# Expert stage of a two-layer encoder trunk: a narrower table of column widths, 4439 columns a layer in place of 4612

## The reference

```
h   = rms_norm(x, norm_mix[l])
x   = x + concat(attention(h), pooling(h), retention(h)) @ w_out[l]
x   = x + moe_ffn(rms_norm(x, norm_ffn[l]), router, w_gate[l], w_up[l], w_down[l])
```

```
layer 0: 127 | 162 157 155 153 153 150 148 142 142 141 139 133 130 130 128 128 127 125 125 113 113 111 111 111 110 110 110 104 104 104 100
layer 1: 137 | 167 167 162 151 150 148 147 144 141 141 138 135 134 130 129 128 128 123 119 118 116 114 113 113 105 104 104 103  98  96  93
```

## Time and profile before

| | |
|---|---|
| median of the runs | 3310.61 us |
| span of the profiled execution | 3312.4 us |
| TensorE busy | 3164.2 us, 96% |
| expert stage, layer 0, first expert matmul to the last one's end | 880.24 to 1650.61 us |
| expert stage, layer 1 | 2529.05 to 3298.26 us |
| HBM read, written | 545.90 MB, 80.35 MB |

### The profile page before, as it was taken

The page is one execution under the profiler, slowest core; times in us unless marked ns, Lnnn a source line. Parts: engine busy times, 40 slices in busy tenths (PEclk is TensorE's granted clock), DMA queues, the critical chain, the costliest instruction groups (busy, mean ns, idle before and its releaser), DMA issues.

```text
span 3312.4 us, 58893 instructions
## 1 busy us (share of the span) xinstructions
PE 3164.2 (96%) x20244; PEld 2476.5 (75%) x20244; DVE 1483.7 (45%) x4546; ACT 627.8 (19%) x1812; POOL 1239.4 (37%) x1346
## 2 busy tenths in 40 slices
PE   7999999998699999999989999999987999999998
PEld 4555556555599999999945565565556999999998
DVE  3576676766322222222236766766763222222221
ACT  4122222222011111111142222221221111111111
POOL 1221321322255545554322322322212554555544
PEclk9999999998899999999989999999988999999999
DMA  7212222123488999999942122122134889999996
GB/s 276 71 55 83 64 62 83 53 73 112 155 277 285 312 306 338 321 339 341 295 146 83 42 83 83 42 83 79 46 125 179 277 282 307 310 335 331 327 342 191
DMA packets 245905, 629.12 MB, mean 190 GB/s; under 512 B 65644, under 2 KB 137836, under 8 KB 212796
## 3 DMA queue, kind: packets, MB, share of 16 engines
q1 hardware_dynamic: 183004, 542.50, 46.1%
q0 software_dynamic: 62592, 82.75, 11.4%
HBM read 545.90 MB, written 80.35 MB: 189 GB/s over the span
## 4 chain that ended last, share of the span: by engine, by line
PE 80%; DMA 6%; DVE 5%; issue 3%; DVEq 2%; ACT 1%; POOL 1%; SPq 1%; ACTq 0%; POOLq 0%
PE bank L1419 23%; PE bank L1226 17%; PE bank L1447 15%; PE bank L1387 12%; DMA arena<-hrows,arena 3%; PE bank L1217 3%; PE bank L1220 3%; PE bank L1190 2%; DVE arena L1135 1%; PE bank L1343 1%; PE bank L1364 1%; PE bank L1288 1%; DMA out<-arena 1%; DMA wts<-in_w_in 1%; DMA arena<-out 1%
## 5 line engine op out<-in xcount | busy, mean ns | idle before, releaser
L1419 PE MATMUL bank<-arena,wts 128*128 128x135 f32 (+6 forms) x8192 | 1023.5, 287 | 3.5 <-ACTq L797 3.5
L1419 PEld LDWEIGHTS bank<-arena,wts 128*128 128x128 f32 x8192 | 1017.1, 191 | 3.7 <-issue 3.7
L1226 PE MATMUL bank<-wts,arena 128*128 128x512 f32 x1536 | 695.1, 599 | 42.2 <-DVEq L879 19.4
L656 POOL DMA_INDIRECT out<-arena x316 | 503.6, 1594 | 204.8 <-ACT arena L806 117.6
L1226 PEld LDWEIGHTS bank<-wts,arena 128*128 128x128 f32 x1536 | 281.9, 192 | 345.5 <-issue 321.2
L1447 PE MATMUL bank<-arena,wts 128*128 128x135 f32 (+6 forms) x4096 | 517.0, 287 | 16.5 <-DVE arena L1168 16.4
L1447 PEld LDWEIGHTS bank<-arena,wts 128*128 128x128 f32 x4096 | 509.3, 190 | 19.7 <-issue 19.7
L1387 PE MATMUL bank<-wts,arena 128*128 128x512 f32 x1024 | 454.5, 597 | 0.0
L646 POOL DMA_INDIRECT arena<-hrows,arena x304 | 296.3, 975 | 187.1 <-issue 169.8
L1387 PEld LDWEIGHTS bank<-wts,arena 128*128 128x128 f32 x1024 | 193.3, 191 | 231.0 <-issue 215.6
L1135 DVE STREAM_TRANSPOSE arena<-arena 128x256 f32<-128x256 f32 x304 | 135.4, 445 | 506.8 <-DMA arena<-hrows,arena 486.5
(11 more groups left out here) (191 smaller groups left out, 2834.2 us busy)
## 6 DMA issues: line engine op xcount, KB each, us to landing
wts<-in_w_gate SPq DMA_DIRECT2D x128, 1024.0 KB, 8.0
wts<-in_w_up SPq DMA_DIRECT2D x128, 1024.0 KB, 10.7
wts<-in_w_down SPq DMA_DIRECT2D x128, 1024.0 KB, 16.0
arena<-out SPq DMA_DIRECT2D x184, 128.0 KB, 3.0
hrows<-arena SPq DMA_DIRECT2D x36, 512.0 KB, 3.9
out<-arena SPq DMA_DIRECT2D x36, 512.0 KB, 2.7
arena<-in_x SPq DMA_DIRECT2D x32, 512.0 KB, 7.0
wts<-in_w_in SPq DMA_DIRECT2D x8, 2048.0 KB, 13.7
```

The lines of the kernel that those rows point to most:

```text
L656: e.indirect_dma_start(opieces, bass.IndirectOffsetOnAxis(ap=piece[:, i, g:g + 1].bitcast(U32), axis=0), ysb[b][:, g * PIECE:(g + 1) * PIE ...
L1226: i = mm(bIP[n % 2][:, :], hT[:, d], win[:, n, d], start=(d == 0), stop=(d == DC - 1))
L1419: return mm(gu_at(f, k, w), lhs, xT[:, d, 0:w], start=start, stop=(d == DC - 1), skip_group_check=True)
```

## The change

```
-WIDTHS = (NT,) * 6 + (160,) * 2 + (155,) * 2 + (150,) * 3 + (140,) * 3 + (135,) * 8 + (P,) * 8
+WIDTHS = (NT,) * 3 + (155,) * 3 + (150,) * 3 + (145,) + (140,) * 3 + (135,) * 3 + (130,) + (P,) * 15
```

## The result

The changed kernel takes 4811.82 us, the median of four runs (4809.93 to 4815.65), against 3311.29 us before (the three runs behind the 3310.61 and a fourth). The ratio is 1.453, with an interval of 1.4511 to 1.4549. The forecast was 4814 us. The stage is narrower, as the change says, and it is run twice in each layer.

A forecast was written before the change was run, and what follows sets the result against it. TensorE was taken as the bound, busy 96%. From a 3312.4 us span, less 2 x 24, plus second rounds with bubbles of 776.4 and 775.2, came 4816, less 1.8: 4814 us; range 4770 to 4880.

The forecast's parts named there:

- The number of rounds: Expert stage: counts exceed the new widths at rank 10 in both layers and rank 3 in layer 1; two rounds each.
- The rival of one round: Both expert stages: counts on the chip fit every new width, so one round each, 3262 us; chance 0.12.
- the one with the saving eaten inside it: Expert stages, one round each: weights arrive too slowly for 128-wide ranks, about 3285 us; chance 0.01.
- that of layer 1 alone: Layer 0's one-token excess vanishes on the chip, so only layer 1 runs two rounds, 4038 us; chance 0.03.
- The saving: Expert matmuls: narrower ranks make each round 24 us shorter, bounded by 20 to 30.
- The second round's price: Expert stage: a second round's matmuls cost those of the first, 746.4 us in layer 0 and 745.2 in layer 1.
- The unknown cost of gathering and adding pads: Second rounds: gathers and additions go to the same few hundred spare rows; -20 to +40 us over both layers.
- the rival above 4880: Second rounds: additions to spare rows get in each other's way, 10% more, about 4960 us; chance 0.03.
- The bubble: Between two rounds: last addition, then slots, rows, transposes and scaling before the first matmul; 30 us, bounds 27 to 38.
- the addend of 2.6: In the gap between rounds: 2.6 us added for expert 0's weights loading late and sharing engines with the row gather.

The follow-up runs named there:

- the last table: Kernel before with widths cut to both layers' counts, 4401 columns, rank 3 at 162, rank 10 at 145: ratio 0.9821, on another chip 3254.99 us, 0.9816.
- the run with two rounds held: Kernel before, old table, with the number of rounds put to two, the second computing pads alone: 4915.75 us, 1.484 of the kernel before.
- the run that parts them: Changed kernel, but in later rounds SyncE issues expert 0's weights only after rank 0's rows arrive: 4818.75 us, 1.455 of the kernel before.
- both mended: Changed kernel with rank 3 at 168 instead of 155 and rank 10 at 145 instead of 140: 3312.23 us, ratio 0.9867; elsewhere 3270.10 us, 0.9864.
- rank 3 alone mended: Changed kernel with rank 3 at 168 instead of 155, rank 10 still at 140: 4904.24 us, 1.460 of the kernel before.
- rank 10 alone: Changed kernel with rank 10 at 145 instead of 140, rank 3 still at 155: 4100.46 us, 1.221 of the kernel before.

## Why the prediction was right

**The number of rounds** was the step that decided, and it could be read neither from the diff nor from the trace. The trace only showed one round a layer, which says nothing of how full the ranks were. It came from putting the reference's inputs through the router and counting. The runs confirm it to a few tokens: with rank 10 at 145 layer 0 runs once, at 140 twice, so it holds 141 to 145 tokens there; in layer 1 either rank alone is enough for a second round, and the last table, which runs once in each layer (8192 records of line 1419) with rank 3 at 162, puts that rank between 156 and 162. No run counts the tokens themselves, so that the excess at rank 10 is one token rests on the reference's counts. The rival of one round (0.12), the one with the saving eaten inside it, and that of layer 1 alone (0.03) fell with the 16384 records of line 1419.

**The saving.** I took 24 us a round from the columns and bounded it by 20 and 30. Against the same layer's round before, the first rounds are 27.6 and 25.5 us shorter and the second ones 24.9 and 22.7 (770.4 - 745.5, 769.2 - 746.5); the mean of the four is 744.6 against 769.8, so 25.2. The columns' part is exact where it can be checked (25.29 at rank 3, 23.69 at width 145). TensorE's idle time at the down matmuls, 8.2 us a round before and 6.0 after, which I had only bounded, adds 2.2: 26.2 in all, 1 us above the mean and within the 22.7 to 27.6 of single rounds.

The 27.7 us that follow for the columns alone from the spacing in the Trainium skill (TensorE: Matmul & The Clock Gate, Back-to-back issue gap) are too much: with the 2.2 us of idle time it would be 29.9, more than any round showed. That formula is the section's gap of an isolated matmul. For a stream of weight loads and matmuls, which this is, the section has about 81 ns at N = 128, and two passes in 111.6 ns do not agree with that either.

**The second round's price** was taken as the first one's, 746.4 and 745.2 us; measured 745.5 and 746.5. The unknown cost of gathering and adding pads, for which I had allowed -20 to +40 us over both layers, is nil within a few us by the run with two rounds held, and the rival above 4880 fell with the result.

**The bubble** was taken as 30 us each, from 27.4 of bare chain plus 2.6 for the company of the weights; measured 31.8 and 30.1. So the addend of 2.6 should have been 4.4 and 2.7. Its cause was half right: the row gather is slower by 2.7 and 3.4 us while the weights are loaded, as the run that parts them shows, but the weights themselves are not waited for.

**A small slip** that cost nothing: I took the run's time to be 1.8 us below the span. Runs of which both are known show it 1.8 us above (4809.93 against 4808.1). The profiled execution before was thus one of 3314.2 us, 3.6 above the median shown, and 4816 + 1.8 - 3.6 gives again 4814.

**How much of the 2 us is luck.** In spans the sum was 4816 against 4808.1, 7.9 us too high: the four rounds saved 4.7 us more than 4 x 24, the bubbles cost 1.9 more than 60, and the stages outside the rounds, which the change does not touch, were 5.1 us shorter. Two thirds of that vanish between the medians, since the profiled execution before was 3.6 us above its median and the one after 1.9 below. The mechanism and the sizes of its terms are borne out; that the forecast is off by 2 us and not by 8 is chance.

## What to carry to other kernels

A table of sizes that data must fit is a cliff: five columns fewer at one of 32 ranks save 0.8 us a round, or cost a whole second round of 777 us, bubble included (745.5 + 31.8). Before such a table is cut, count the data, in every layer, and compare rank by rank; no profile of a run that fits shows how near the edge it is. And a busy share of 96% on the bounding engine before and after hid that the share of padding grew from 11% of the expert stage's columns (8192 pairs in 2 x 4612) to 54% (8192 in 4 x 4439); the count of instructions shows the doubling at once.

## What was not expected of the hardware

- A chip on which the kernel before took 3358.05 us (median of seven, 3354.3 to 3360.1) where it took 3311 to 3314 on the others, 1.4% more at nearly the same granted clock (0.977 to 0.979 there, 0.978 to 0.981 elsewhere). With both mended, rounds took 761.9 us there and 748.1 us elsewhere, and the mixing stage between the layers 883.1 against 877.0. TensorE was held 30 times, 13.5 us in all, inside line 1419, with no producer to be seen in the profile. That is not all of it: its busy time in a round was longer too, 751.9 and 754.4 us against 740.9 and 740.5 for the same table elsewhere. With rank 3 alone mended the transposes of line 1410 were held as well (18.8 us in 31 pieces), and the bubbles were 38.7 and 38.9 us; with rank 10 alone the one bubble was 32.9 us. The kernel before has no trace from that chip, and what is slow there stays open.
- One run in nine of the last table took 7070.67 us, about 3770 more than the others, with a granted clock of 1.000. It did not come again in five runs on another chip. Whether it was the chip or a number of rounds gone wrong isn't known, as no trace of it exists. Added rounds would fit badly: one costs about 790 us on that chip (755 + 33), so 3770 us are 4.8 of them, and two added rounds leave the mean granted clock at 0.980 (the run with two rounds held), not at 1.000.
